# Recurrence gates of a hybrid encoder on one Trainium2 core: four 64x64 tile products side by side in place of 128x128 products

## The reference

```python
xb = xf.reshape(bsz, t, LRU_HEADS, LRU_BLOCK)
r = jax.nn.sigmoid(jnp.einsum('bthi,hij->bthj', xb, w_a).reshape(bsz, t, LRU_WIDTH) + b_a)
i = jax.nn.sigmoid(jnp.einsum('bthi,hij->bthj', xb, w_x).reshape(bsz, t, LRU_WIDTH) + b_x)
log_a = -LRU_C * r * jax.nn.softplus(-lam)
a = jnp.exp(log_a)
gated_x = jnp.sqrt(-jnp.expm1(2.0 * log_a)) * (i * xf)
```

## Time and profile before

| | us |
|---|---|
| median of 3 runs | 1355.46 (1355.41 to 1356.73) |
| span of the profiled execution, first to last instruction | 1354.8 |
| PE busy | 1325.8 (98%) |
| DVE busy | 855.6 (63%) |
| ACT busy | 434.6 (32%) |
| POOL busy | 331.1 (24%) |

### The profile page before, as it was taken

One profiled execution on the slowest core, in us unless ns is written; L12 is line 12 of the kernel. 1 busy time (PEld: TensorE's weight loads), 2 busy tenths in 40 slices (PEclk: granted clock), 3 DMA queues, 4 the chain that ended last, 5 costly groups with the idle time before them and its releaser, 6 DMA issues.

```text
span 1354.8 us, 27409 instructions
## 1 busy us (share of the span) xinstructions
PE 1325.8 (98%) x11200; PEld 904.0 (67%) x11200; DVE 855.6 (63%) x1939; ACT 434.6 (32%) x1044; POOL 331.1 (24%) x450
## 2 busy tenths in 40 slices
PE   5999999999999999999999999999999999999997
PEld 3577776666654454667877788877788777875543
DVE  3847874355454375785886858858578586782246
ACT  3213443344431233521422414224143241432221
POOL 1023200010013232523312423224222242212352
PEclk9999999999999999999999999999999999999999
DMA  9531016002034522121212112121121211440124
GB/s 356 235 75 36 5 36 271 8 1 79 3 130 167 195 85 108 13 81 19 71 46 68 34 34 83 38 77 40 34 83 29 75 50 34 127 159 26 35 94 168
DMA packets 63297, 111.96 MB, mean 83 GB/s; under 512 B 34778, under 2 KB 38690, under 8 KB 61618
## 3 DMA queue, kind: packets, MB, share of 16 engines
q1 hardware_dynamic: 63172, 110.21, 24.2%
HBM read 91.79 MB, written 18.40 MB: 81 GB/s over the span
## 4 chain that ended last, share of the span: by engine, by line
PE 88%; DVE 7%; POOL 1%; DMA 1%; issue 1%; ACT 1%; SPq 0%; DVEq 0%; POOLq 0%; ACTq 0%
PE psum L1132 83%; PE psum L1135 5%; DVE mem L2963 1%; DVE mem L2774 1%; DVE mem L3288 1%; DMA mem<-x_dram 1%; DVE mem L3054 0%; DMA y<-mem 0%; DVE mem L3165 0%; DVE mem L2943 0%; DMA mem<-x 0%; POOL mem L954 0%; DVE mem L2780 0%; ACT mem L1915 0%; ACT mem L2087 0%
## 5 line engine op out<-in xcount | busy, mean ns | idle before, releaser
L1132 PE MATMUL psum<-mem 32*32 32x32 f32 (+12 forms) x10592 | 1264.1, 304 | 4.9 <-DVE mem L2475 1.5
L1132 PEld LDWEIGHTS psum<-mem 128*128 128x128 f32 (+4 forms) x10592 | 835.7, 143 | 401.7 <-issue 217.0
L2963 DVE SCALAR_TENSOR_TENSOR mem<-mem 128x576 f32<-128x576 f32 (+1 forms) x126 | 106.1, 842 | 0.0
L1135 PE MATMUL psum<-mem 128*128 128x128 f32 (+1 forms) x608 | 85.1, 278 | 17.2 <-ACT mem L1927 12.9
L1135 PEld LDWEIGHTS psum<-mem 128*128 128x128 f32 (+1 forms) x608 | 70.7, 144 | 41.4 <-issue 21.0
L2278 ACT ACTIVATE mem<-mem 128x128 f32<-128x128 f32 x72 | 22.0, 305 | 127.6 <-DVE mem L3213 74.4
L2164 ACT ACTIVATE mem<-psum 128x288 f32<-128x288 f32 x28 | 11.4, 407 | 104.0 <-PE psum L1132 104.0
L1011 POOL COPY mem<-mem 128x3 f32<-128x3 f32 x24 | 8.4, 348 | 148.9 <-DVE mem L2921 70.1
L2056 ACT ACTIVATE mem<-mem 128x256 f32<-128x256 f32 x72 | 35.5, 495 | 26.4 <-DVE mem L2697 26.4
L2744 DVE TENSOR_TENSOR mem<-mem,psum 128x512 f32<-128x512 f32 x28 | 19.1, 684 | 37.4 <-PE psum L1132 37.0
L2174 ACT ACTIVATE mem<-mem 128x576 f32<-128x576 f32 (+1 forms) x42 | 32.7, 779 | 28.0 <-DVE mem L2941 28.0
(11 more groups left out here) (260 smaller groups left out, 1277.2 us busy)
## 6 DMA issues: line engine op xcount, KB each, us to landing
mem<-modw SPq DMA_DIRECT2D x12, 2048.0 KB, 12.2
mem<-w SPq DMA_DIRECT2D x44, 512.0 KB, 4.3
mem<-x SPq DMA_DIRECT2D x10, 512.0 KB, 4.7
x_dram<-mem SPq DMA_DIRECT2D x9, 512.0 KB, 2.9
mem<-row_dram SPq DMA_DIRECT2D x8, 576.0 KB, 5.2
mem<-x_dram SPq DMA_DIRECT2D x9, 512.0 KB, 3.7
mem<-wout SPq DMA_DIRECT2D x1, 4096.0 KB, 15.0
mem<-gs SPq DMA_DIRECT2D x8, 512.0 KB, 3.6
```

The costliest lines, as they stand in the source:

```text
L1132: return pe.matmul(*a, **k)
L1135: return pe.transpose(out, in_, ident[0:n, 0:n])
L2963: x = dve.scalar_tensor_tensor(cvm, U1[:, m, lo + j:hi + j], CW[:, 3 * g + ORDER[m], j:j + 1], cvm, ALU.mult, ALU.add)
```

## The change

The six 128x128 products of a round become three thirds. A third makes both gates for 384 columns with four 64x64 products, one on each quarter of the array: gate a's two blocks read the input where it lies and write bank 6, gate x's two blocks write bank 7 and read a copy of the input with its two 64-partition halves exchanged. Two DMAs on SP's queue make this copy, once `xc_ready` is there, in a row of YT that is free at the time. `gw` keeps only the nonzero blocks and comes in four DMAs of 64 partitions by 64 numbers. All six DMAs count on `gw_in`, and PE waits for all of them. The first third stands where the gates stood. The other two stand behind the first and the second part of the following pair (in round 3: before the second and third projection group). ACT evicts in the order third by third, a then x; its wait for `l_y` is now ahead of the second eviction of the round, where it was ahead of the fourth.

```diff
+XS_ROW = (2, 2, 7, 7)
...
-        gw = take(2, P)
+        gw = take(P)
...
+            def swapped(m):
+
+                sp.wait_ge(sem("xc_ready"), m + 1)
+                if m >= 2:
+                    sp.wait_ge(sem("st_mm"), STEPS * 2)
+                for r, s in ((slice(0, 64), slice(64, P)), (slice(64, P), slice(0, 64))):
+                    sp.dma_start(YT[r, XS_ROW[m]], xc[s]).then_inc(sem("gw_in"), 16)
+
             for m in range(LM):
                 if m:
-                    sp.wait_ge(sem("l_mm"), 6 * m)
-                sp.dma_start(gw, I["gw"][m]).then_inc(sem("gw_in"), 16)
+                    sp.wait_ge(sem("l_mm"), 3 * m)
+                for q in range(2):
+                    for s in range(2):
+                        r = slice(64 * s, 64 * s + 64)
+                        cols = slice(64 * (s ^ q), 64 * (s ^ q) + 64)
+                        sp.dma_start(gw[r, cols], I["gw"][m, cols, q, cols]).then_inc(sem("gw_in"), 16)
+                swapped(m)
...
-            def pair(p):
+            def pair(p, between=None):
...
                 for j in range(2):
                     freed(j, 0, "u4")
                     part("1", j, w1, 0, HT, 0, lo(j))
+                    if between:
+                        between(j + 1)
...
             def gates(m):
-                pe.wait_ge(sem("gw_in"), 16 * m + 16)
+                halves = slice(0, 64), slice(64, P)
+
+                def third(n):
+
+                    if m or n:
+                        pe.wait_ge(sem("lz_ev"), 6 * m + 2 * n)
+                    t = slice(n * NC, n * NC + NC)
+                    for q, src in enumerate((xc, YT[:, XS_ROW[m]])):
+                        for s, r in enumerate(halves):
+                            cols = halves[s ^ q]
+                            i = mm(B(6 + q)[cols, 0:NC], gw[r, cols], src[r, t], start=True, stop=True)
+                    i.then_inc(sem("l_mm"), 1)
+
+                pe.wait_ge(sem("gw_in"), 96 * m + 96)
                 pe.wait_ge(sem("xc_ready"), m + 1)
                 if m == 0:
                     pe.wait_ge(sem("mod_done"), 1)
-                for i in range(6):
-                    if m or i >= 2:
-                        pe.wait_ge(sem("lz_ev"), 6 * m + i - 1)
-                    mm(B(6 + i % 2)[:, 0:NC], gw[:, i // 3], xc[:, (i % 3) * NC:(i % 3 + 1) * NC],
-                       start=True, stop=True).then_inc(sem("l_mm"), 1)
+                third(0)
                 if m < LM - 1:
-                    pair(m + 1)
+                    pair(m + 1, third)
                     return
                 for q in range(2):
                     pe.wait_ge(sem(f"w0_in{q}"), 16 * m + 48)
-                    project(m, q, "g_mm", lambda n: pe.wait_ge(
-                        sem("st_add"), STEPS * (PAIRS - 1) + LAST_FREE[3 * q + n]))
+
+                    def freed(n):
+
+                        if q == 0 and n:
+                            third(n)
+                        pe.wait_ge(sem("st_add"), STEPS * (PAIRS - 1) + LAST_FREE[3 * q + n])
+
+                    project(m, q, "g_mm", freed)
...
             def lru(m):
...
-                for i in range(6):
-                    wait(act, sem("l_mm"), 6 * m + i + 1)
-                    if m and i == 0:
-                        wait(act, sem("l_a"), m)
-                    elif m and i == 3:
-                        wait(act, sem("l_y"), m)
-                    dst = (tr, ti)[i // 3][:, (i % 3) * NC:(i % 3 + 1) * NC]
-                    act.activation(dst, B(6 + i % 2)[:, 0:NC], ACT.Tanh, scale=0.5,
-                                   bias=gbias[:, m, i // 3:i // 3 + 1]).then_inc(sem("lz_ev"), 1)
-                wait(act, sem("lz_ev"), 6 * m + 3)
+                for n in range(3):
+                    wait(act, sem("l_mm"), 3 * m + n + 1)
+                    for q, dst in enumerate((tr, ti)):
+                        if m and n == 0:
+                            wait(act, sem("l_y" if q else "l_a"), m)
+                        act.activation(dst[:, n * NC:(n + 1) * NC], B(6 + q)[:, 0:NC], ACT.Tanh, scale=0.5,
+                                       bias=gbias[:, m, q:q + 1]).then_inc(sem("lz_ev"), 1)
+                wait(act, sem("lz_ev"), 6 * m + 5)
...
                 if m:
-                    dve.wait_ge(sem("l_mm"), 6 * m)
+                    dve.wait_ge(sem("l_mm"), 3 * m)
```

## The result

The kernel after takes **1365.91 us** (median of 4 runs, 1363.71 to 1367.8) against 1355.76 of the kernel before beside it: a ratio of 1.0075, 95% interval 1.0063 to 1.0088. Slower by 10 us, where 1355.9 with a range up to 1361.2 was predicted. The profiled execution took 1364.86 us, its span is 1362.7.

What follows compares the result with a forecast made beforehand. PE was taken as the bound before, the loop through ACT, DVE and the exchange after: +1.9 us over three rounds, less 1.5 in the last, total +0.4, so 1355.9 us predicted, range 1352.3 to 1361.2.

Steps and rivals of the forecast that it cites:

- Part 1: Tile products on PE: four abreast, a third 0.98 us, a round 2.94 against 4.47; PE alone gains 6.1 us in all.
- the sum: Whole stage: three rounds 96.8 us against 94.9, so +1.9; the last round gains 1.5; total +0.4 us.
- Rival C: Tiles on PE do not run abreast: +7.8 us, 1363.7, if a bank's two take turns; 1379 if fully serial; chance 0.06.
- Part 2: Loop through ACT and DVE: L2600 (now L2629) at 10.4 us, 2.7 later; then 17.9, 18.4, 17.3 us to xc_ready.
- Part 3: Exchanged halves: two DMAs issued at xc_ready take 4.0 us until PE can start, bounds 2.9 and 5.1.
- an exchange on the path: Between xc_ready and a round's first third: the exchange's 4.0 us added in full to each of rounds 0 to 2.
- Part 4: Second eviction waits for l_y: third 1 may start 6.9 us after xc_ready, no added stall; a slow L2649 costs 1.0.
- The last round: Round 3, gates and projections: no gates behind it, so it gains 1.5 us.
- `wqkv`: Weight load in round 3: lands at 32.8 us against PE's arrival at 33.9, so it holds by 1.1 us.
- the single loop: ACT, DVE, exchange added as one chain: rounds of 32.3, 32.8 and 31.7 us over PE's own 30.1.
- Rival A: Slow exchange, at PE's wait for gw_in: 5.1 us gives +3.7, 1359.2; with POOL's full cost +5.9, 1361.4; chance 0.27.
- Rival B: Loop does not bind, PE keeps all its 6.1 us: 1349.4; a milder form 1352.6; chance 0.17, mostly mild.

Runs made afterwards that it cites:

- e11: e6 with two whole 128x128 products for a third instead of four tiles, and no exchange: 1359.54 us, ratio 1.0023.
- e6: e5 with the thirds nearer to each other (2.43 us apart, not 2.94) and the last pair's c12 additions ahead of l_y: 1353.59 us, ratio 0.9984.
- e10: The changed kernel with the thirds 2.43 us apart instead of 2.94, nothing else: 1360.46 us, ratio 1.0032.
- e12: e6 with c21 additions ahead of c22 gate products, the exchange cut in two by columns, and the second third behind the whole first group: 1353.29 us, ratio 0.9977.
- e14: e12 without the exchange, so some products have wrong inputs: 1352.55 us, ratio 0.9976.
- e1: The changed kernel with POOL's weight sums of pairs 2 and 3 waiting for xc_ready, so after the scans: 1365.91 us, ratio 1.0076.
- e2: The changed kernel without the exchange, so some products have wrong inputs: 1366.82 us, ratio 1.0078.
- e7: e5 without the exchange, so some products have wrong inputs: 1363.78 us, ratio 1.0057.
- e15: The changed kernel with each exchange sent a second time once the first has landed: 1387.24 us, ratio 1.0236.
- e13: The kernel before, with the first gate product of rounds 1 to 3 also waiting for the last pair's c12 additions: 1365.69 us, ratio 1.0077.
- e9: The changed kernel with the last pair's c12 additions ahead of l_y, nothing else: 1365.93 us, ratio 1.0069.
- e3: The changed kernel with the three thirds together ahead of the pair, tiles and exchange kept: 1363.15 us, ratio 1.0054.
- e8: The kernel before with the late weight sums of e1 alone: 1355.36 us, ratio 0.9995.
- e5: e1 with the scan written over its own input, and the wait for l_y moved from the eviction to L2629: 1360.92 us, ratio 1.0034.

## Why the prediction was wrong

**Part 1 held.** A third's eight records take 0.88 us (the row at 206.99), so the four tiles of bank 6 and 7 ran side by side. By starts a third costs 1.00 us, against 0.98 in the sum; these are the weight loads of round 0's first two thirds, 2.94 us apart with a part of 1.94 between them:

```profile
104.43 0.21 PEld L1146 LDWEIGHTS psum<-mem 64*64 64x64 f32 x8 [0.39 <-issue]
...
107.37 0.21 PEld L1146 LDWEIGHTS psum<-mem 64*64 64x64 f32 x8 [0.39 <-issue]
```

Rival C asked for a third of 1.6 us. The Trainium skill, page "TensorEngine Tiling (Array Packing)", section "Restrictions and Gotchas", says that different row tiles cannot access the same PSUM bank at the same time. The trace does not agree: within these 0.88 us two row tiles wrote each bank, in different partitions of it. e11 against e6 prices tiles with exchange at 5.3 us, and the stages of e6, e10, e12 and e14 say that 5.3 to 5.5 of the predicted 6.1 are kept.

**Part 2 held in the time of L2629** (10.4 predicted, 10.4 to 10.5 measured) **and failed in the stretch behind it.** The prediction said "Whether the scan suffers no row shows" and took half of POOL's old 2.2 us, with 2.2 as its upper end. The scans suffer more than the convolution did: a short instruction is held for a whole sum. 19.62 and 20.37 against 17.9 and 18.4: 3.7 us. e1 shows what the stretch is without the sums, 16.46 and 17.31, so they cost 3.2 and 3.1 us, where the prediction's upper end was 2.2.

**Part 3 was 0.6 short and wrong in kind.** From `xc_ready` to the first third it is 4.6 us, not 4.0, inside the bounds: 1.9 us in three rounds. But the step "an exchange on the path" fell. e2, e7 and e14 take it away and gain nothing, because the c21 additions and tanh hold the first eviction and, in the changed kernel, `l_y` the second. Part 4 had seen the second of these for rounds 1 and 2, the first not at all. Of the exchange only 0.43 us was exposed on ACT at round 1; e15 shows that there was no room beyond it.

**The last round** was to gain 1.5 and lost 1.3. The sum took the 1.5 in full, and so left out a queue that the thirds uncover: the last pair's c12 additions stand behind `l_y` on DVE, and 4.47 us of gate products used to cover them (e13, in the kernel before, shows them 0.75 us behind PE's arrival at these gates). With one third (0.9 us) in front of the projections they come 1.15 us too late. Another 1.7 us is the half-clock stretch at 209.5. Together 2.85 us, the whole miss of this term of the sum. `wqkv` held, as predicted, with no wait of `kv`.

The three misses, 3.7 + 1.9 + 2.85 on a predicted +0.4, make 8.85, and 0.2 comes from the three stretches up to L2629: 9.05 against the 9.06 measured. So in size the terms that failed are the DVE stretch, the exchange and the last round. **In kind, the failed step is the single loop**: the sum added the links ACT, DVE, exchange as one chain and took every other wait as covered. The runs show several chains of nearly one length into the same turn: the exchange, c21's tanh (0.43 us short of it on ACT), `l_y` behind that, and c11 or c12 into PE's next work. That is why three single repairs (e1, e2, e9) returned nothing and all together (e6) 12.3 us. The clock has a share in this: the profiles of these three have 3.4 to 6.8 us more at 1.2 GHz than that of the changed kernel. That the exchange is hidden doesn't rest on it, since third 1 begins at the same time with and without (e2, e7) and e14 has no such stretch. Only nearer thirds paid alone: 2.8 us with all three together (e3), 5.4 with 0.5 us less between them (e10). That this is because they shorten every chain at once is my reading; what the trace shows is the squared decay sooner and the scans of round 0 clear of the sums.

The loop that was added up did bind the changed kernel's rounds: PE waits for the exchange at each first third, and L2629 for ACT. What the sum could not say is what a shorter link would give back.

Rival A named a condition that was met: it decides "from 4.1 with POOL's full cost", the exchange took 4.6, and POOL cost more than that full cost. With 4.6 and 2.2 its sum is +4.4 us, 1359.9. The rest is POOL beyond 2.2 us a round and the last round, which A did not name. Rival B's full gain of 6.1 is about what PE saved, not what it kept.

What stays open is when the clock falls. The profiles of before, e6, e8, e12 and e14 have no stretch at 1.2 GHz in the stage. Of the thirteen others eleven have some; e10 and e13, with 10.0 and 6.5 us of PE waits, have none. No run separates what the waits did from where in time they fell, and how much of each median is the clock's is known for the profiled execution alone.

## What to carry to other kernels

- Before work is moved off a dense stretch of the bounding engine, list every queue that this stretch covered: not only the wait that is moved, but each instruction that lies between the producer and its consumer on the other engines, here c12 behind `l_y` and the evictions behind c21's tanh. Price each chain from its own start, and take the longest at each turn; a repair of one of several equal chains shows nothing, which is no proof that it was harmless.
- Split work into pieces as near to each other as the evictions allow (2.0 to 2.4 us here), since the consumer starts from the last piece; and look at what a shifted engine comes to lie beside.

## What the runs showed that was not expected

- Short VectorE scans (128x16, 0.22 us) beside GpSimd's 128x512 additions take up to 1.30 us, one whole addition (1.26), while the additions lose nothing; eight of them went from 1.25 to 4.42 us.
- Four 64x64 tiles that write two banks, two row tiles into each, ran abreast: 0.88 us from first start to last end, and 1.00 from start to start with the switch of form included, for a set that would take 2.58 one after another.
- Two 64-partition DMAs within the on-chip memory, 576 KB together, reach PE 4.6 us after their semaphore; a second pair behind the first costs the like again (e15).
- PE waits of one length came with the lower clock in some profiles and without it in others (2.11 us in the changed kernel with it, 2.12 in e13 without); the changed kernel's own runs spread over 4 us, those of e6 over 1.8.
- The time from a profile's first instruction to the start of the stage differs by up to 2 us between profiles, so the length of a stage is taken between two marks of its own. An end counted from the first instruction made e5 look 2.1 us better than it is.
